# Putting expert slot rows back to their tokens with TensorE products for all eight positions, instead of DRAM rows and indirect transfers

## The reference, cut to what matters

```python
logits = (hf @ w_r) + b_r
top_v, top_i = lax.top_k(logits, 2)
gates = jax.nn.softmax(top_v, axis=-1)
combine = sum(one_hot(top_i, 8) * gates[..., None], axis=-2)
for e in range(8):
    out = out + combine[:, e:e+1] * ((silu(hf @ w1[e]) * (hf @ w3[e])) @ w2[e])   # w1, w3: 1024x2816, w2: 2816x1024
x = x + g2 * out
return rmsnorm(x, final_g)
```

## Time and profile before

| what | us |
|---|---|
| median of 3 runs | 1485.72 |
| lowest, highest | 1484.06, 1485.72 |
| the profiled execution, its own time | 1484.85 |
| its span in the profile | 1483.0 |
| PE busy | 1384.1 (93%) |
| DVE busy | 525.7 (35%) |
| ACT busy | 398.7 (27%) |
| GpSimd busy | 4.1 |
| moved by DMA | 395.92 MB, mean 267 GB/s |

### The profile page before, as it was taken

One profiled execution on the slowest core, in us unless ns is written; L12 is line 12 of the kernel. 1 busy time (PEld: TensorE's weight loads), 2 busy tenths in 40 slices (PEclk: granted clock), 3 DMA queues, 4 the chain that ended last, 5 costly groups with the idle time before them and its releaser, 6 DMA issues.

```text
span 1483.0 us, 25756 instructions
## 1 busy us (share of the span) xinstructions
PE 1384.1 (93%) x11327; PEld 821.8 (55%) x11327; DVE 525.7 (35%) x954; ACT 398.7 (27%) x701; POOL 4.1 (0%) x8
## 2 busy tenths in 40 slices
PE   6899889999999999989898999999999998889886
PEld 3688657888888888878675343333333332223221
DVE  2799884523232333469864112011100010001022
ACT  3522485422222322376482111010110010000001
POOL 0000000000000000000000000000000000000010
PEclk9999899999999999999999999999999999999898
DMA  9997903532331052411418999999999999999995
GB/s 353 385 343 274 352 2 114 171 114 68 103 114 57 29 187 97 143 57 58 171 41 341 399 371 409 406 409 406 409 407 408 408 406 410 405 410 406 408 410 221
DMA packets 147031, 395.92 MB, mean 267 GB/s; under 512 B 7488, under 2 KB 38752, under 8 KB 146912
## 3 DMA queue, kind: packets, MB, share of 16 engines
q1 hardware_dynamic: 144000, 388.86, 68.7%
q10 hardware_dynamic: 2336, 3.24, 0.6%
q0 software_dynamic: 576, 2.10, 0.4%
HBM read 390.76 MB, written 3.41 MB: 266 GB/s over the span
## 4 chain that ended last, share of the span: by engine, by line
PE 77%; DMA 12%; DVE 6%; SPq 2%; ACT 2%; issue 1%; DVEq 0%; ACTq 0%
PE bank L1196 22%; DMA weight_ring<-in_exp_w 9%; PE bank L1154 8%; PE bank L1013 5%; PE bank L1014 5%; PE bank L1012 5%; PE bank L735 4%; PE bank L736 4%; PE bank L737 4%; DMA weight_ring<-in_w_ada 3%; PE bank L1021 3%; PE bank L1022 3%; PE bank L1023 3%; PE bank L1162 2%; PE bank L681 2%; DVE weight_ring L1865 2%
## 5 line engine op out<-in xcount | busy, mean ns | idle before, releaser
L1196 PE MATMUL bank<-weight_ring,gathered 128*32 128x512 f32 (+1 forms) x3840 | 402.2, 569 | 32.9 <-DMA weight_ring<-in_exp_w 27.1
L1196 PEld LDWEIGHTS bank<-weight_ring,gathered 128*32 128x32 f32 x3840 | 127.0, 112 | 283.0 <-issue 282.3
L2259 DVE TENSOR_TENSOR scratch<-scratch,bank 64x512 f32<-64x512 f32 (+1 forms) x60 | 38.4, 640 | 357.2 <-ACT scratch L1672 354.9
L1154 PE MATMUL bank<-weight_ring,scratch 128*32 128x512 f32 x1344 | 157.8, 593 | 2.2 <-DMA weight_ring<-in_exp_w 2.2
L1014 PE MATMUL bank<-slot_halves,slot_halves 128*128 128x512 f32 x336 | 130.9, 390 | 0.0
L1013 PE MATMUL bank<-hT_halves,slot_halves 128*128 128x512 f32 x336 | 130.9, 390 | 0.0
L1012 PE MATMUL bank<-slot_halves 128*128 128x512 f32 x320 | 124.8, 390 | 0.0
L1865 DVE SCALAR_TENSOR_TENSOR weight_ring<-scratch,conv_weights,weight_ring 128x512 f32<-128x512 f32 (+1 forms) x207 | 121.3, 637 | 2.6 <-ACT weight_ring L1453 0.7
L736 PE MATMUL bank<-hT_halves,slot_halves 128*128 128x512 f32 (+1 forms) x352 | 122.0, 347 | 0.0
L735 PE MATMUL bank<-slot_halves,slot_halves 128*128 128x512 f32 (+1 forms) x284 | 105.6, 372 | 8.1 <-DVE slot_halves L1772 5.2
L1154 PEld LDWEIGHTS bank<-weight_ring,scratch 128*32 128x32 f32 x1344 | 43.8, 110 | 100.3 <-issue 91.0
(11 more groups left out here) (303 smaller groups left out, 1576.1 us busy)
## 6 DMA issues: line engine op xcount, KB each, us to landing
weight_ring<-in_exp_w SPq DMA_DIRECT2D x216, 1024.0 KB, 18.5
weight_ring<-in_w_ada SPq DMA_DIRECT2D x24, 2048.0 KB, 13.5
weight_ring<-in_exp_w SPq DMA_DIRECT2D x64, 768.0 KB, 15.0
weight_ring<-in_ffn_w SPq DMA_DIRECT2D x33, 1024.0 KB, 5.4
weight_ring<-in_w_in SPq DMA_DIRECT2D x8, 1024.0 KB, 11.6
weight_ring<-in_w_out SPq DMA_DIRECT2D x4, 2048.0 KB, 11.2
weight_ring<-in_w_in SPq DMA_DIRECT2D x2, 3072.0 KB, 15.2
expert_rows<-scratch ACTq DMA_DIRECT2D x14, 128.0 KB, 6.0
```

The source lines that it names most:

```text
L1154: i = mm(bank[6][quarter, :], at01[:, c0:c0 + BLOCK], w2[:, i_, half * 512:(half + 1) * 512], start=(first and i_ == 0), stop=(last and i_ ...
L1196: i = mm(ps[BLOCK * job:BLOCK * (job + 1), 0:cw], gathered_block(e, k, b), w[:, kk, a * cw:(a + 1) * cw], start=(k == 0), stop=(k == KT - 1))
```

## The change

The rows of all eight positions are put back by PE in the way position 7's were. For position e-1, in step g = 3e+1: DVE makes the selection matrices (`select_slots`, two instructions for small and four for large positions), PE transposes them after pair 0 into a bank of step g-1 that is free, ACT copies them (`slots_copied`), PE multiplies them with the scaled rows after pair 2 (tokens 0 to 127) and after pair 3 (tokens 128 to 255), and DVE adds the four results to `ftok`, scaled by that position's gate. Large positions have a second pair of products for the third block, 32 rows deep, accumulated in the same banks. The second scatter waits until the first two results are added, as both use the same two banks; step 3e+2 waits until all four are. For position 7 the transposes move from step 22 to step 23; its scatter stays in the tail. The DRAM tensor, ACT's 22 writes, the search for rows, the four indirect transfers with GpSimd's whole program, and the four additions of fetched rows go. The gathers that used the same banks move: those of positions 2 and 3 all to step 5, those of step 10 to step 9. Instead of two tables per expert and the gate of the last position, DVE computes the gates of all positions (`gates_of_positions`).

```diff
-FILL_STEPS = [None, None, [(4, 0), (4, 1), (5, 0), (5, 1)],
-              [(g, p) for g in (10, 11) for p in range(4)]]
+FILL_STEPS = [None, None, [(5, p) for p in range(4)],
+              [(g, p) for g in (9, 11) for p in range(4)]]
...
-            def scatter(n):
+            def slots_of_tokens(r, e, ps):
+                pe.wait_ge(slot_sel, NE * r + e + 1)
+                for z in range(BLOCKS_OF[e] - 1):
+                    for n in range(2):
+                        i = pe.transpose(ps[:, (2 * z + n) * P:(2 * z + n + 1) * P], sel_slots[z][n], ident)
+                i.then_inc(slot_mm, 1)
+
+            def scatter(r, e, n, banks):
+                pe.wait_ge(slot_ready, NE * r + e + 1)
+                pe.wait_ge(yt_ready, before(e, r, 1, 2) + BLOCKS_OF[e] - 1)
+                small = e in SMALL
                 for half in range(2):
                     part = slice(HD * half, HD * half + HD)
-                    mm(bank[SCATTER_BANK[2 * n + half]][:, :], to_token[part, n, :], rows_01[part, :],
-                       start=True, stop=True).then_inc(scatter_mm, 1)
+                    i = mm(banks[half][:, :], to_token[part, n, :], rows_01[part, :], start=True, stop=small)
+                    if small:
+                        i.then_inc(scatter_mm, 1)
+                if not small:
+                    for half in range(2):
+                        part = slice(HD * half, HD * half + BLOCK)
+                        mm(banks[half][:, :], to_token_2[part, n, :], rows_2[part, :],
+                           start=False, stop=True).then_inc(scatter_mm, 1)
...
+                    if e and j == 2:
+                        pe.wait_ge(scatter_added, scatters_before(e, r))
...
+                        if e and j == 1:
+                            spare_banks = [sums(g - 1, 2), sums(g - 1, 1)]
+                            if p == 0:
+                                slots_of_tokens(r, e - 1, spare_banks[0])
+                            elif p == 2:
+                                if e not in SMALL:
+                                    pe.wait_ge(a_t2, before_group(g - 1, r, 0, 1) + 1)
+                                scatter(r, e - 1, 0, spare_banks)
+                            elif p == 3:
+                                pe.wait_ge(scatter_added, scatters_before(e - 1, r) + 2)
+                                scatter(r, e - 1, 1, spare_banks)
+                        if g == NG - 1 and p == 1:
+                            slots_of_tokens(r, e, sums(g - 1, 2))
...
-                for i in range(4):
-                    pool.indirect_dma_start(chosen[i], None, rows_kept[:, :],
-                                            bass.IndirectOffsetOnAxis(ap=row_at[:, i:i + 1], axis=0)
-                                            ).then_inc(row_back, 16)
...
-                        act.dma_start(rows_kept[at:at + n, half * 512:(half + 1) * 512],
-                                      rows_[HD * half:HD * half + n, :]).then_inc(row_kept, 16)
...
+                def slots_copied(e):
+                    act.wait_ge(slot_mm, NE * r + e + 1)
+                    if NE * r + e:
+                        act.wait_ge(scatter_mm, scatters_before(e, r))
+                    n = 2 * P * (BLOCKS_OF[e] - 1)
+                    f(slots_turned[:, 0:n], slot_bank(e)[:, 0:n],
+                      ACT.Copy).then_inc(slot_ready, 1)
...
                     if e and j == 1:
+                        select_slots(e - 1)
                         rows_scaled(e - 1, r)
...
-                    elif g == 8:
-                        rows_found(r)
-                    elif g == 16:
-                        select_last()
-                    elif g == NG - 1:
+                    if e and j == 1:
                         for i_ in range(4):
-                            choice_added(r, i_)
+                            add(r, e - 1, i_, [sums(g - 1, 2), sums(g - 1, 1)])
+                    if g == NG - 1:
+                        select_slots(NE - 1)
                     gated(g)
```

More of the change, by code:

```diff
@@ L105, in slots @@
     return BLOCK * BLOCKS_OF[i]
-def first_row(i):
-    return sum(slots(p) for p in range(i))
 def before(i, r, small, large):
@@ L522, in backbone, with slot_bank, scatters_before @@
         SCATTER_BANK = [0, 1, 2, 5]
-        def kept_before(i, r):
-            each = [32 if p in SMALL else 64 for p in range(NE - 1)]
-            return r * sum(each) + sum(each[:i])
+        def slot_bank(e):
+            return sums(CH * e + CH if e < NE - 1 else NG - 2, 2)
+        def scatters_before(i, r):
+            return 4 * (NE * r + i)
         pv = posm[:, 0:2 * NE].rearrange("p (e n) -> p e n", n=2)
         cv = comb[:, 0:2 * NE].rearrange("p (e n) -> p e n", n=2)
-        placed, gate_last = (att[:, a:a + n].rearrange("p (e n) -> p e n", n=2) for a, n in ((16, 2 * NE), (32, 2)))
+        placed, gate_at = (att[:, a:a + 2 * NE].rearrange("p (e n) -> p e n", n=2) for a in (16, 80))
         of_position = scr[:, 7424:7488].rearrange("p (i e) -> p i e", e=NE)
         parts = scr[:, 7488:7616]
-        key, rank, held_by, at_position, over, slots_by, line_by = (att[:, 40 + i * NE:48 + i * NE] for i in range(7))
+        key, rank, held_by, at_position, over = (att[:, 40 + i * NE:48 + i * NE] for i in range(5))
         def rounds(eng, body, end):
@@ L1203, in expert_steps @@
                 if r and begin == 0:
[L1204 to L1205 removed]
+                    pe.wait_ge(scatter_added, scatters_before(0, r))
                 if begin == 0:
@@ L1266, in last_scatter @@
                     second_unit(r, NG - 1, u)
-                pe.wait_ge(yt_ready, before(0, r + 1, 1, 2))
                 for n in range(2):
-                    scatter(n)
+                    scatter(r, NE - 1, n, [bank[b] for b in SCATTER_BANK[2 * n:2 * n + 2]])
             rounds(pe, experts, last_scatter)
[L1274 to L1278, removed]
-                for i in range(4):
-                    pool.indirect_dma_start(chosen[i], None, rows_kept[:, :],
-                                            bass.IndirectOffsetOnAxis(ap=row_at[:, i:i + 1], axis=0)
-                                            ).then_inc(row_back, 16)
-            rounds(pool, rows_fetched, lambda r, last: None)
         @block.scalar
@@ L2199, in choice_added, with add @@
-            def choice_added(r, i):
-                v, n = divmod(i, 2)
-                dve.wait_ge(row_back, 64 * (r + 1))
-                if v:
-                    dve.wait_ge(row_added, 4 * r + n + 1)
+            def add(r, e, i_, banks):
+                n, half = divmod(i_, 2)
+                dve.wait_ge(scatter_mm, scatters_before(e, r) + i_ + 1)
+                if NE * r + e:
+                    dve.wait_ge(scatter_added, scatters_before(e, r))
                 else:
                     dve.wait_ge(row_copied, 5)
-                    if r:
-                        dve.wait_ge(scatter_added, 4 * r)
-                row = scr[:, 2048 + n * D:2048 + (n + 1) * D]
-                stt(out=row, in0=chosen[i], scalar=share[:, i:i + 1], in1=row,
-                    op0=ALU.mult, op1=ALU.add).then_inc(row_added, 1)
@@ L2213, in add @@
[L2213 to L2216 removed]
                 dst = ftok[:, n, half, :]
[L2218 removed]
+                stt(out=dst, in0=banks[half][:, :], scalar=gate_at[:, e, n:n + 1], in1=dst,
                     op0=ALU.mult, op1=ALU.add).then_inc(scatter_added, 1)
@@ L2305, in last_rows @@
                 for i_ in range(4):
-                    add(r, i_)
+                    add(r, NE - 1, i_, [bank[b] for b in SCATTER_BANK[2 * (i_ // 2):2 * (i_ // 2) + 2]])
                 if last:
@@ L2361, in tables @@
     for row in (np.where(np.arange(NE) == 0, -4096, np.arange(NE)), RANK_OF_POSITION,
-                [slots(i) for i in range(NE)], [first_row(i) for i in range(NE)]):
+                [slots(i) for i in range(NE)]):
         cols.append(np.broadcast_to(np.asarray(row, np.float32), (P, NE)))
```

123 lines of the change are left out of this document (33 added, 90 removed).

## The result

The changed kernel takes 1474.83 us (median of 6 runs, 1473.67 to 1476.46), the kernel before 1484.36 us in 6 runs beside it (1483.32 to 1485.72). The ratio is 0.9936 with a 95% interval of [0.9926, 0.9945]: 9.5 us faster. The profiled execution took 1474.66 us, with a span of 1472.9 us, 10.1 less than before.

A forecast was written before the change was run, and what follows sets the result against it. The prediction took the never-idle DMA weight stream as the bound: writes 5.8 + reads 5.1 = 10.9 us removed, PE's added work covered, so 1484.85 - 10.9 = 1473.95, by the median 1474.8 us; range 1472.5 to 1480.5.

The forecast's parts named there:

- the sum: Whole kernel: 10.9 us less on the path, all else covered, giving 1473.95 us, by the median 1474.8; chance 60%.
- What bounds it: Expert stage: the stream of weights by DMA, never idle at 407 to 409 GB/s, sets the end, not PE.
- rival B: Expert stage: PE bound in part, overrunning by 2 to 8 us; gain only 3 to 9 us, 1476.7 to 1482.7; chance 15%.
- rival D: DMA queue: no change in time, as the removed bytes ran in holes; chance 5%.
- The traffic: DMA queue: 2.36 MB of writes and 2.10 MB of reads removed, 5.8 + 5.1 = 10.9 us at 409 GB/s.
- PE's new work: Positions 0 to 6: products and transposes, 2.3 us per small and 4.4 per large position, 24.5 us added on PE.
- rival A: Positions 0 to 6: paired halves run one behind the other, PE becomes the bound, 3.1 us slower, 1488.8 us; chance 7%.
- Does that fit: Expert stage: PE's added work fits into its waits in both legs, DMA staying the bound with PE 2 to 5 us inside.
- the ledger: PE's added work and the earlier stream against PE's spare time: 3 us over up to 1310.8 us, 1.9 after.
- The ring: Weight buffer, step 4: PE 4.4 us later holds back SP's transfers; put at nothing, bounds 0 and 4.4 us.
- Waits added: New products: PE's waits for DVE and ACT are covered, `gated` in step 4 having 7.1 us of cover against 3.4.
- Rival C: Last two units: PE with less idle keeps its clock, gaining 1.9 us more, 1472.9 us; chance 13%.

## Why the prediction was right

The forecast was 1474.8 us, from the sum -10.9; the median is 1474.83. Point by point:

- **What bounds it.** Right. The edits that put bytes back and those that took them out of the kernel before all moved the time, while 26 us of PE work taken out moved it by 1.3 us, not clear of nothing, and left the stage as long as it was to 0.2 us. So rival B, PE bound in part, falls, and with the edits that moved bytes rival D.
- **The traffic, -10.9 us.** Right in kind. The two halves measured 5.2 + 5.2 = 10.4 on the kernel before, against 5.8 + 5.1, and 9.2 when both were put back on the changed one. All lie within 2 us of the sum by bytes, and the stage of the changed kernel with both put back is 10.5 us longer. The 17 us for the writes was an estimate from the Trainium skill's table ("DMA: Bandwidth & Descriptors", Bandwidth), which is for transfers to SBUF that GpSimd issued. The measurement decides: beside this full stream the writes cost 5.2 us.
- **PE's new work, 24.5 us.** Undersized by 2 us. A set of two products took 1.06 us between the stream's products, not 0.86 to 1.0. A large position cost 4 x 1.06 + 0.53 = 4.8, not 4.4, a small one 2 x 1.06 + 0.37 = 2.5, not 2.3: 26.6 us before rounding. The halves do run in pairs, so rival A has no ground.
- **Does that fit.** It did, with more room than the 2 to 5 us of the ledger. 7.1 us of waits were left, and the doubled products found 9 to 10 us early, and at least 6 late. Two things were left out of the ledger. Step 21's first pair and turn took 9.34 us before (1379.52 to 1388.86), at low clock and with a second stop of 1.37 us, and 6.45 in the changed kernel: 2.9 us. And each wait is worth some 0.19 us more than the list gives it.
- **The ring, put at nothing.** Right as far as the end goes: 405 in place of 407 GB/s in 860 to 1130, worth 1.3 us, but without the products the stage is no shorter. That a late PE can starve the queue is shown by the kernel with early products doubled (398 GB/s).
- **Waits added.** Right: none of the new products waited for DVE or ACT, and the gathers' move showed no cost. `gated` of step 4 ended 4.8 us later than before (930.95 in place of 926.18), within the 7.1 us of cover.
- **The sum** lands on the median more closely than its parts deserve. I subtracted it from 1485.72, the median of three runs; over six runs that median is 1484.36, 1.4 us lower. And the gain was 9.5 us, 1.4 us smaller than the sum. The two errors offset each other, and that the forecast meets the median to 0.03 us is luck. The gain's own interval, 8.2 to 11.0 us, just holds the 10.9. In the profiled executions the stage was 11.6 us shorter, 10.5 without the low clock at the end of before, so the sum itself was good to 0.4 us.
- **Rival C.** The tail did run at a clock of 1.00 in 1456 to 1462, as C said, but not for its reason. The kernel before with its gathers moved waits for weights nearly as long as the kernel before (23.0 + 6.0 = 29.0 us from 860 to 1475, against 27.1 + 5.4 = 32.5), and its last two units (timeline of PE, first two rows) take 1.92 us each, full speed. And the changed kernel with the reads put back stood 2.00 us ahead of its last unit but one, just as before did, and kept its clock (third row):

```profile
1465.97 1.92 PE L1154 MATMUL bank<-weight_ring,gathered 128*32 128x512 f32 x16 [1.36 <-DMA weight_ring<-in_exp_w]
1468.92 1.92 PE L1154 MATMUL bank<-weight_ring,gathered 128*32 128x512 f32 x16 [1.03 <-DMA weight_ring<-in_exp_w]
...
1463.04 1.92 PE L1159 MATMUL bank<-weight_ring,gathered 128*32 128x512 f32 x16 [2.00 <-DMA weight_ring<-in_exp_w]
```

So the slow last units of before belonged to that execution, and C's 1.9 us are not what the change gives back; only 1.1 us of them came behind the last landing. Nor does the clock as a whole explain the times: with both put back its mean over the program is 0.979 (median of 11 runs), the kernel before has 0.973, and they take the same time. The prediction counted the 0.66 of 1374 to 1389 among the falls behind waits for DMA; what stands ahead of it is the stop of 4.43 us at the branch.

## What to carry to other kernels

Where the DMA queue was full for a whole stage, as here, every byte moved in it was time at the end, at the stream's own rate, in transfers of 64 to 512 KB and however well their latency was hidden; look for scratch writes, read-backs and broadcasts there, and ask which engine with idle time could do the same. Make a ledger of that engine's idle time between the points where it catches up with the stream, since time given away before a catch-up is free and time behind the last one is not. Test both sides: put the bytes back on the new kernel, and double the new work until it shows. And measure the stage that was changed by itself in the profiles: what scatters ahead of it here (2.5 us) is a quarter of the gain.

## What the runs showed that I had not expected

- A set of two products costs 1.06 us when something of another shape follows, and 0.86 when its like follows: the two sets of the tail take 1.99 us together, of which the last one has 1.13, its length in the timeline. The difference of 0.2 us is about one weight load (182 to 187 ns each). The sets that are only 32 rows deep (line 1131) take 1.06 us as well: a shallower product is no cheaper.
- PE stands 4.4 to 4.7 us at the branch between steps 20 and 21 in every profile, whether it arrives early or late. The granted clock of 1374 to 1389, around and behind this stop, is 0.66 in four kernels (before, its gathers moved, its writes left out, and the changed one without the products), 0.77 in the changed one and in the three with bytes put back, and 0.89 in the two with the final row spread, with the late products doubled, and also in the kernel before without its reads. That last one waits for weights about as long as the kernel before (31.4 us against 32.5), so idle time alone doesn't set it; the cause stays open. (With the early products doubled it is 1.00, as the stop comes later there, up to 1390.33.)
- PE was idle for 1.5 us in 1311 to 1374 of the changed kernel (busy 61.51 of 63.00 us), and no wait for weights accounts for it. It is the head of the stop at the branch, which began at 1372.51 (1377.09 - 4.58). A stretch cut across a wait shows idle time that isn't room.
